# The matmuls of a gate tile and its up tile in alternating order, in the up projections of a transformer block

## The chip, the cores and the metric

The kernel runs on one core of a Trainium2 chip. Five engines work side by side and meet at semaphores: TensorE (PE, matmuls), VectorE (DVE), ScalarE (ACT), GpSimd (POOL) and SyncE (SP, which issues most transfers). The metric is the device time of one execution in microseconds (us), lower is better; a kernel's time is the median of its runs.

## The reference

Two blocks follow each other on a sequence of 512 tokens with 1024 features, in float32: one with two feed-forward networks around a mixer (attention over selected keys, and retention), and one with gated linear attention and a third feed-forward network. This case is about the three feed-forward networks. Each has two wide matrices side by side, "gate" and "up" (1024 to 2816 features), and a "down" matrix back to 1024. The third has a causal convolution of width 3 over the tokens ahead of the gating.

```
def swiglu(x, w_gate, w_up, w_down):
    return (jax.nn.silu(x @ w_gate) * (x @ w_up)) @ w_down
...
h = h + 0.5 * swiglu(rms_norm(h, ffn1_norm[i]), ffn1_w_gate[i], ffn1_w_up[i], ffn1_w_down[i])
...
def conv_ffn(x, w_up, conv_w, conv_b, w_down):
    s = x.shape[1]
    u = x @ w_up
    u_pad = jnp.pad(u, ((0, 0), (CONV_WIDTH - 1, 0), (0, 0)))
    u = sum(u_pad[:, j:j + s] * conv_w[j] for j in range(CONV_WIDTH)) + conv_b
    gate, up = jnp.split(u, 2, axis=-1)
    return (jax.nn.silu(gate) * up) @ w_down
```

## The kernel before, in words

Activations lie in SBUF with features on the 128 partitions and the 512 tokens along the row. All matmuls of the projections are made of three: operands are split into a high part (rounded to the matmul's format) and a low part (the rest), and the products low x high, high x low and high x high are added up in one PSUM bank (`mm3`, lines 1352 to 1357; the line of a matmul in the profile is one of 1355, 1356 and 1357 wherever it was called from).

A *slab* is the block of weights of one output tile: 8 blocks of 128 x 128, 512 KB. A ring of 4 slots (`RING`) holds raw slabs, their high parts and their low parts. SP loads raw slab n when the low part of slab n-4 is made. ACT makes the high part (line 613) when the raw slab has landed and the tile that used slab n-4 is done. POOL makes the low part (line 536) after it and increments `lo_ready`, on which TensorE waits. A *tile* is 128 output features x 512 tokens, 24 matmuls of 512 columns, in one of 4 PSUM banks (`BANKS`) in rotation; its last matmul increments `tile_done`, and the evacuation by DVE increments `tile_freed`, on which the tile four later waits.

An up projection (`ffn_up` in the program of the tensor engine) has 44 tiles, gate and up in turn, so 22 pairs. The first four tiles are written out; the others run in a loop of 10 rounds. The normalization is applied at the evacuation: the matmuls work on x times the gain, whose chunks are released by `u_ready`, and the factor `rstd` comes later, from a matmul with ones over the sums of squares (`sums(k)`), a root on ACT (line 639) and some steps on DVE (lines 905 to 914). `sums` stands behind tile 1 in the first up projection (k = 0) and behind tile 0 in the others (k = 2 and 5).

For a pair, DVE evacuates gate (line 927) and up (929), multiplies (932) after ACT's Silu (653), and makes the low part of the hidden chunk (934) after ACT's copy to its high part (656). In the third up projection DVE's list is longer, for gate and for up each: evacuation (951) and three steps of the convolution (953, 956, 959); then the product (963) and the low part (965). ACT's order in a pair p (`pair`, lines 645 to 657) is: the high part of slab 2p+4, Silu of the gate, the copy of the hidden chunk, the high part of slab 2p+5. After the 44 tiles the down projection (8 tiles of 66 matmuls, three slabs each) starts; it needs the first 18 hidden chunks at its start, and the last four one by one.

Every engine runs its own program in order; nothing reorders the matmuls.

Of the kernel before, what the change touches and what calls it, by code (L numbers as in the profile page):

```python
# [27 lines left out]
KD = D // P  # L28
# [15 lines left out]
RING = 4  # L44
BANKS = 4
# [135 lines left out]
def layer_program(nc, A, out):  # L181
# [12 lines left out]
    with ExitStack() as ctx:  # L194
# [8 lines left out]
        w_hi = sb("w_hi", [P, RING, SLAB], F32R)  # L203
        w_lo = sb("w_lo", [P, RING, SLAB], F32R)
        h = sb("h", [P, KD, S])
        u_hi = sb("u_hi", [P, KD, S], F32R)
        u_lo = sb("u_lo", [P, KD, S], F32R)
# [71 lines left out]
        acc = ctx.enter_context(nc.psum_tensor("acc", [P, BANKS, S], F32))  # L279
# [15 lines left out]
        lo_ready = sem("lo_ready")  # L295
        slab_used = sem("slab_used")
        tile_done = sem("tile_done")
        tile_freed = sem("tile_freed")

        u_hi_ready = sem("u_hi_ready")  # L300
        u_ready = sem("u_ready")
# [123 lines left out]
        def blk(b):  # L425
            return slice(b * P, (b + 1) * P)
# [909 lines left out]
        def _(pe):  # L1336
# [6 lines left out]
            def slabs_ready(n):  # L1343
                pe.wait_ge(lo_ready, n + 1)

            def free_bank(t):

                if t >= BANKS:
                    pe.wait_ge(tile_freed, t - BANKS + 1)
                return acc[:, t % BANKS, :]  # L1350

            def mm3(o, w, x_hi, x_lo, first, last):

                slot, columns = w
                pe.matmul(o, w_lo[:, slot, columns], x_hi, start=first, stop=False)  # L1355
                pe.matmul(o, w_hi[:, slot, columns], x_lo, start=False, stop=False)  # L1356
                return pe.matmul(o, w_hi[:, slot, columns], x_hi, start=False, stop=last)  # L1357
# [18 lines left out]
            def fm_tile(t, blocks, x_hi, x_lo, ready=None):  # L1376

                o = free_bank(t)
                seen = None
                for k, (n, b) in enumerate(blocks):  # L1380
                    if n != seen:
                        slabs_ready(n)
                        seen = n
                    if ready is not None:
                        pe.wait_ge(*ready(k))
                    last = mm3(o, (n % RING, blk(b)), x_hi[:, k, :], x_lo[:, k, :], k == 0, k == len(blocks) - 1)
                last.then_inc(tile_done, 1)
# [16 lines left out]
            def ffn_up(k, name):  # L1404

                n0, t0 = plan.first[name]
                for j in range(RING):
                    fm_tile(t0 + j, [(n0 + j, b) for b in range(KD)], u_hi, u_lo, (lambda c: (u_ready, KD * k + c + 1)) if j == 0 else None)
                    if j == (1 if k == 0 else 0):
                        sums(k)  # L1410
                with pe.Fori(1, 2 * KF // RING) as i:
                    for j in range(RING):
                        pe.wait_ge(lo_ready, i * RING + (n0 + j + 1))
                        pe.wait_ge(tile_freed, i * RING + (t0 + j - BANKS + 1))
                        for b in range(KD):
                            last = mm3(acc[:, (t0 + j) % BANKS, :], ((n0 + j) % RING, blk(b)), u_hi[:, b, :], u_lo[:, b, :], b == 0, b == KD - 1)
                        last.then_inc(tile_done, 1)

            def ffn_down(f, name):

# [22 lines left out]
            for step in MIX:  # L1443
# [5 lines left out]
                elif kind == "avw":  # L1449
                    o = free_bank(t)  # L1450
                    slabs_ready(n)
                    for k in range(KD):
                        last = mm3(o[0:AVW, :], (n % RING, slice(k * AVW, (k + 1) * AVW)), u_hi[:, k, :], u_lo[:, k, :], k == 0, k == KD - 1)
                    last.then_inc(tile_done, 1)
                elif kind == "avt":
# [3 lines left out]
                    for tt in range(NT):  # L1459
                        last = pe.transpose(aux[:, 3, tt * AVW:(tt + 1) * AVW], y_sq[0:AVW, 0, blk(tt)], ident[0:AVW, 0:AVW])  # L1460
# [6 lines left out]
                elif kind == "index":  # L1467
                    b = step[1]
# [3 lines left out]
                    for hd in range(2 * step[2], 2 * step[2] + 2):  # L1472
                        j = index_units[b] + hd
# [291 lines left out]
```

## Time and profile before

| | before |
|---|---|
| median of 3 runs | 1982.21 us (1982.18 to 1983.98) |
| profiled execution, span | 1981.7 us |
| PE busy | 95% (8492 matmuls, 8492 weight loads) |
| DVE / ACT / POOL busy | 49% / 35% / 43% |
| granted TensorE clock, mean | 0.977 |
| first / second / third up projection | about 8.5 to 256, 913 to 1154, 1579 to 1839 us |

The three up projections take 38% of the span. Busy shares are averages over stages: DVE is busy for about half of the kernel, but for 8 tenths and more of each slice in the third up projection. A matmul's busy time in the profile is longer than the distance to the next one, since they are pipelined; the pace is read from the starts.

### The profile page before, as it was taken

The page shows a single profiled execution, that of the slowest core. Times are in us where ns is not written, and L with a number is a line of the kernel's source. Part 1 is how long each engine was busy: PE and PEld are TensorE (multiplying, and loading weights), DVE is VectorE, ACT ScalarE, POOL GpSimd, SP SyncE. Part 2 cuts the span into 40 slices and gives each one's busy share as a digit, 9 for nine tenths or more (in the row PEclk, how much of TensorE's full clock was granted, in tenths as well). Part 3 has the DMA queues.
Part 4 walks back from the last instruction along what each step waited for, and adds up shares of the span by engine and source line. Part 5 has one row for each costly group of instructions (what it writes and reads, how often), then busy time and mean ns, then how long its engine had stood idle before and what let it go on. Part 6 is the DMA issues. An engine that isn't in the chain of part 4 may idle for free.

```text
span 1981.7 us, 23231 instructions
## 1 busy us (share of the span) xinstructions
PE 1884.6 (95%) x8492; PEld 1501.5 (76%) x8492; DVE 979.0 (49%) x1318; ACT 702.8 (35%) x923; POOL 842.3 (43%) x391
## 2 busy tenths in 40 slices
PE   7999999998889789999999999998999999999996
PEld 5888888786767457878888888876877887777785
DVE  6222244426777744334222222377756388888413
ACT  6434323313222444224443422335344433333221
POOL 4444444394547413444444444432333433344541
PEclk9999999998999899999999999998999999999998
DMA  4332333252222201222323233312222222222331
GB/s 165 105 106 86 101 95 95 85 154 70 80 69 71 79 32 64 96 85 96 102 89 106 84 98 97 103 55 84 72 69 66 94 85 85 85 85 82 109 95 43
DMA packets 52527, 174.52 MB, mean 88 GB/s; under 512 B 6368, under 2 KB 6752, under 8 KB 52464
## 3 DMA queue, kind: packets, MB, share of 16 engines
q1 hardware_dynamic: 52320, 173.40, 27.0%
q8 instruction: 41, 0.67, 0.1%
q10 hardware_dynamic: 144, 0.26, 0.0%
q14 instruction: 22, 0.18, 0.0%
HBM read 166.56 MB, written 2.10 MB: 85 GB/s over the span
## 4 chain that ended last, share of the span: by engine, by line
PE 61%; issue 21%; POOL 8%; DVE 7%; ACT 2%; DMA 0%; POOLq 0%; SPq 0%; DVEq 0%; ACTq 0%
PE acc L1355 19%; PE acc L1357 19%; PE acc L1356 18%; POOL w_lo L536 7%; PE acc L1538 1%; PE aux L1514 1%; PE aux L1495 1%; ACT w_hi L613 1%; DVE bias L1075 1%; DVE small L1074 1%; DVE y_sq L910 1%; PE aux L1476 0%; DVE probs L1114 0%; PE aux L1528 0%; DVE bias L1064 0%
## 5 line engine op out<-in xcount | busy, mean ns | idle before, releaser
L536 POOL TENSOR_TENSOR w_lo<-w_raw,w_hi 128x1024 fp32r<-128x1024 f32 (+1 forms) x317 | 754.1, 2384 | 1092.6 <-ACT w_hi L613 1092.5
L1355 PE MATMUL acc<-u_hi,w_lo 128*128 128x512 f32 x1592 | 634.6, 399 | 31.6 <-POOL w_lo L536 16.0
L1356 PE MATMUL acc<-u_lo,w_hi 128*128 128x512 f32 x1592 | 625.4, 393 | 0.0
L1357 PE MATMUL acc<-u_hi,w_hi 128*128 128x512 f32 x1592 | 625.0, 393 | 0.0
L613 ACT ACTIVATE w_hi<-w_raw 128x1024 fp32r<-128x1024 f32 (+1 forms) x317 | 325.0, 1034 | 566.9 <-PE acc L1357 506.8
L1355 PEld LDWEIGHTS acc<-u_hi,w_lo 128*128 128x128 f32 x1592 | 301.3, 189 | 114.6 <-issue 39.6
L1357 PEld LDWEIGHTS acc<-u_hi,w_hi 128*128 128x128 f32 x1592 | 300.7, 189 | 65.6 <-issue 0.8
L1356 PEld LDWEIGHTS acc<-u_lo,w_hi 128*128 128x128 f32 x1592 | 301.2, 189 | 64.3 <-issue 2.5
L1355 PE MATMUL acc<-hid_hi,w_lo 128*128 128x512 f32 x528 | 207.3, 393 | 2.1 <-POOL w_lo L536 2.1
L1357 PE MATMUL acc<-hid_hi,w_hi 128*128 128x512 f32 x528 | 207.3, 393 | 0.0
L1356 PE MATMUL acc<-hid_lo,w_hi 128*128 128x512 f32 x528 | 205.6, 389 | 0.0
L656 ACT ACTIVATE hid_hi<-tmp 128x512 f32 (+1 forms) x66 | 41.7, 632 | 272.5 <-DVE tmp L932 199.4
L989 DVE SCALAR_TENSOR_TENSOR h<-acc,h 128x512 f32<-128x512 f32 x24 | 16.6, 692 | 225.2 <-PE acc L1357 225.2
L929 DVE TENSOR_TENSOR tmp<-acc,rstd 128x512 f32<-128x512 f32 x44 | 30.4, 691 | 192.1 <-PE acc L1357 192.1
L1355 PEld LDWEIGHTS acc<-hid_hi,w_lo 128*128 128x128 f32 x528 | 99.2, 188 | 23.4 <-POOL w_lo L536 2.9
L1356 PEld LDWEIGHTS acc<-hid_lo,w_hi 128*128 128x128 f32 x528 | 99.1, 188 | 22.4
L1357 PEld LDWEIGHTS acc<-hid_hi,w_hi 128*128 128x128 f32 x528 | 99.2, 188 | 22.1
L956 DVE SCALAR_TENSOR_TENSOR tmp<-tmp,cols 128x512 f32<-128x512 f32 x44 | 72.4, 1647 | 6.6 <-DVE tmp L953 5.0
L927 DVE TENSOR_TENSOR tmp<-acc,rstd 128x512 f32<-128x512 f32 x44 | 30.4, 691 | 91.6 <-PE acc L1357 91.2
L1399 PE MATMUL acc<-w_hi,u_lo 128*128 128x256 f32 x256 | 72.9, 285 | 0.0
L1400 PE MATMUL acc<-w_lo,u_hi 128*128 128x256 f32 x256 | 72.4, 283 | 0.0
L1401 PE MATMUL acc<-w_hi,u_hi 128*128 128x256 f32 x256 | 72.4, 283 | 0.0
(271 smaller groups left out, 2115.9 us busy)
## 6 DMA issues: line engine op xcount, KB each, us to landing
w_raw<-in_w_up SPq DMA_DIRECT2D x132, 512.0 KB, 3.4
w_raw<-in_w_mix SPq DMA_DIRECT2D x69, 512.0 KB, 3.6
w_raw<-in_w_down SPq DMA_DIRECT2D x48, 512.0 KB, 3.5
w_raw<-in_w_gla SPq DMA_DIRECT2D x32, 512.0 KB, 3.4
w_raw<-in_w_down SPq DMA_DIRECT2D x24, 384.0 KB, 3.1
w_raw<-in_w_ple SPq DMA_DIRECT2D x10, 512.0 KB, 3.5
tmp<-tmp SPq DMA_DIRECT2D x36, 64.0 KB, 2.0
h<-in_xT SPq DMA_DIRECT2D x8, 256.0 KB, 6.0
```

Source lines behind the costliest of these rows:

```text
L536: pool.tensor_tensor(w_lo[:, slot, 0:width], w_raw[:, slot, 0:width], w_hi[:, slot, 0:width].bitcast(F32), ALU.subtract).then_inc(lo_ready, 1)
L613: act.activation(w_hi[:, slot, 0:width], w_raw[:, slot, 0:width], ACT.Copy).then_inc(hi_ready, 1)
L656: act.activation(hid_hi[:, i2 + b, :], src, ACT.Copy).then_inc(prod_hi, 1)
L927: dve.tensor_tensor(gate_t[:, b, :], acc[:, (t0 + 2 * b) % BANKS, :], rstd[:, :], ALU.mult).then_inc(tile_freed, 1)
L929: dve.tensor_tensor(up_t[:, b, :], acc[:, (t0 + 2 * b + 1) % BANKS, :], rstd[:, :], ALU.mult).then_inc(tile_freed, 1)
L956: dve.scalar_tensor_tensor(tmp[:, part, :], z[:, 1:1 + S], conv_col("conv_w1", i * 2, b, part * KF), tmp[:, part, :], ALU.mult, ALU.add).t ...
L1355: pe.matmul(o, w_lo[:, slot, columns], x_hi, start=first, stop=False)
L1356: pe.matmul(o, w_hi[:, slot, columns], x_lo, start=False, stop=False)
L1357: return pe.matmul(o, w_hi[:, slot, columns], x_hi, start=False, stop=last)
L1399: pe.matmul(o, u_lo[:, k, blk(tt)], w_hi[:, slot, columns], start=k == 0, stop=False)
L1400: pe.matmul(o, u_hi[:, k, blk(tt)], w_lo[:, slot, columns], start=False, stop=False)
L1401: last = pe.matmul(o, u_hi[:, k, blk(tt)], w_hi[:, slot, columns], start=False, stop=k == KD - 1)
```

## The change

Tiles are taken in pairs (0, 1) and (2, 3) of each round. For a pair, TensorE first waits for both slabs and both banks, and then issues, for each of the 8 blocks and each of the three products, one matmul of the gate tile and one of the up tile, in their two banks. Each tile's own matmuls keep their order. In the first up projection the first pair keeps the old order; in the others it alternates too, with the waits for the chunks of u, and `sums` then comes behind the pair. The last two matmuls of a pair release the two tiles. Nothing is changed on the other engines.

```
             def ffn_up(k, name):
 
                 n0, t0 = plan.first[name]
-                for j in range(RING):
-                    fm_tile(t0 + j, [(n0 + j, b) for b in range(KD)], u_hi, u_lo, (lambda c: (u_ready, KD * k + c + 1)) if j == 0 else None)
-                    if j == (1 if k == 0 else 0):
+
+                def pair_tiles(j, ready=None):
+                    for b in range(KD):
+                        if ready is not None:
+                            pe.wait_ge(u_ready, ready + b + 1)
+                        for part, operand, start, stop in ((w_lo, u_hi, b == 0, False), (w_hi, u_lo, False, False), (w_hi, u_hi, False, b == KD - 1)):
+                            for e in (j, j + 1):
+                                ins = pe.matmul(acc[:, (t0 + e) % BANKS, :], part[:, (n0 + e) % RING, blk(b)], operand[:, b, :], start=start, stop=stop)
+                                if stop:
+                                    ins.then_inc(tile_done, 1)
+
+                for j in (0, 2):
+                    if j == 0 and k == 0:
+                        for e in range(2):
+                            fm_tile(t0 + e, [(n0 + e, b) for b in range(KD)], u_hi, u_lo, (lambda c: (u_ready, c + 1)) if e == 0 else None)
+                    else:
+                        for e in (j, j + 1):
+                            slabs_ready(n0 + e)
+                            free_bank(t0 + e)
+                        pair_tiles(j, KD * k if j == 0 else None)
+                    if j == 0:
                         sums(k)
                 with pe.Fori(1, 2 * KF // RING) as i:
-                    for j in range(RING):
-                        pe.wait_ge(lo_ready, i * RING + (n0 + j + 1))
-                        pe.wait_ge(tile_freed, i * RING + (t0 + j - BANKS + 1))
-                        for b in range(KD):
-                            last = mm3(acc[:, (t0 + j) % BANKS, :], ((n0 + j) % RING, blk(b)), u_hi[:, b, :], u_lo[:, b, :], b == 0, b == KD - 1)
-                        last.then_inc(tile_done, 1)
+                    for j in (0, 2):
+                        for e in (j, j + 1):
+                            pe.wait_ge(lo_ready, i * RING + (n0 + e + 1))
+                            pe.wait_ge(tile_freed, i * RING + (t0 + e - BANKS + 1))
+                        pair_tiles(j)
```

## Rows read from the trace of the kernel before

**Rows 1.** The page, chain of work that ended last: share of each line.

```profile
PE acc L1355 19%; PE acc L1357 19%; PE acc L1356 18%; POOL w_lo L536 7%; PE acc L1538 1%; PE aux L1514 1%; PE aux L1495 1%; ACT w_hi L613 1%; DVE bias L1075 1%; DVE small L1074 1%; DVE y_sq L910 1%; PE aux L1476 0%; DVE probs L1114 0%; PE aux L1528 0%; DVE bias L1064 0%
```

**Rows 2.** Order of time, PE (start, duration, engine, operation): 256 columns, up2's tiles 4 and 43.

```profile
435.24 0.28 PE L1399 MATMUL acc<-w_hi,u_lo 128*128 128x256 f32 x1
435.36 0.28 PE L1400 MATMUL acc<-w_lo,u_hi 128*128 128x256 f32 x1
...
935.95 0.39 PE L1355 MATMUL acc<-u_hi,w_lo 128*128 128x512 f32 x1
...
1148.11 0.39 PE L1355 MATMUL acc<-u_hi,w_lo 128*128 128x512 f32 x1
```

**Rows 3.** Order of time, DVE and POOL, up2 under way: released together by tile_done.

```profile
963.35 0.69 DVE L927 TENSOR_TENSOR tmp<-acc,rstd 128x512 f32<-128x512 f32 x1 [2.31 <-PE acc L1357]
...
964.49 2.39 POOL L536 TENSOR_TENSOR w_lo<-w_raw,w_hi 128x1024 fp32r<-128x1024 f32 x1 [0.89 <-ACT w_hi L613]
```

**Rows 4.** Order of time, up2's entry: first evacuation, and slabs 5 and 6.

```profile
927.99 0.69 DVE L927 TENSOR_TENSOR tmp<-acc,rstd 128x512 f32<-128x512 f32 x1 [0.22 <-DVE rstd L914]
...
931.87 4.76 POOL L536 TENSOR_TENSOR w_lo<-w_raw,w_hi 128x1024 fp32r<-128x1024 f32 x2 [6.56 <-ACT w_hi L613]
```

**Rows 5.** Order of time, up1's entry: sums, tile 4; slab 3, slabs 5 to 8.

```profile
24.90 1.70 PE L1363 MATMUL aux<-ssum,ones 128*128 128x512 f32 x2 [2.37 <-DVE ssum L901]
...
38.40 0.39 PE L1355 MATMUL acc<-u_hi,w_lo 128*128 128x512 f32 x1
...
24.94 2.35 POOL L536 TENSOR_TENSOR w_lo<-w_raw,w_hi 128x1024 fp32r<-128x1024 f32 x1 [3.03 <-ACT w_hi L613]
...
40.08 10.47 POOL L536 TENSOR_TENSOR w_lo<-w_raw,w_hi 128x1024 fp32r<-128x1024 f32 x4 [6.57 <-ACT w_hi L613]
```

**Rows 6.** Order of time, up3's entry: evacuation, convolution; tile 4; slabs 5 and 6.

```profile
1593.39 0.69 DVE L951 TENSOR_TENSOR tmp<-acc,rstd 128x512 f32<-128x512 f32 x1
...
1595.08 0.75 DVE L956 SCALAR_TENSOR_TENSOR tmp<-tmp,cols 128x512 f32<-128x512 f32 x1 [0.16 <-DVE tmp L953]
...
1601.33 0.39 PE L1355 MATMUL acc<-u_hi,w_lo 128*128 128x512 f32 x1
...
1602.41 4.95 POOL L536 TENSOR_TENSOR w_lo<-w_raw,w_hi 128x1024 fp32r<-128x1024 f32 x2 [11.71 <-ACT w_hi L613]
```

**Rows 7.** Order of time, up3: DVE; POOL; PE's tile 11 and down's 25th matmul.

```profile
1599.92 0.69 DVE L963 TENSOR_TENSOR tmp<-tmp 128x512 f32<-128x512 f32 x1
...
1602.15 0.69 DVE L951 TENSOR_TENSOR tmp<-acc,rstd 128x512 f32<-128x512 f32 x1
...
1605.25 2.65 DVE L956 SCALAR_TENSOR_TENSOR tmp<-tmp,cols 128x512 f32<-128x512 f32 x1 [0.15 <-DVE tmp L953]
...
1611.97 0.69 DVE L963 TENSOR_TENSOR tmp<-tmp 128x512 f32<-128x512 f32 x1
...
1614.46 4.94 POOL L536 TENSOR_TENSOR w_lo<-w_raw,w_hi 128x1024 fp32r<-128x1024 f32 x2 [7.11 <-ACT w_hi L613]
...
1638.56 2.38 POOL L536 TENSOR_TENSOR w_lo<-w_raw,w_hi 128x1024 fp32r<-128x1024 f32 x1 [7.11 <-ACT w_hi L613]
...
1641.07 0.49 PE L1355 MATMUL acc<-u_hi,w_lo 128*128 128x512 f32 x1 [0.87 <-POOL w_lo L536]
...
1845.46 0.51 PE L1355 MATMUL acc<-hid_hi,w_lo 128*128 128x512 f32 x1 [0.60 <-POOL w_lo L536]
```

**Rows 8.** PE after two idles; stretches: PE, PEld, DVE, ACT, POOL busy, clock, DMA.

```profile
874.02 0.50 PE L1355 MATMUL acc<-mg_hi,w_lo 128*128 128x512 f32 x1 [1.53 <-DVE mg_lo L998]
...
1293.13 0.79 PE L1355 MATMUL acc<-p_hi,w_lo 128*128 128x512 f32 x1 [3.94 <-DVE tmp L1187]
...
25.00:28.50 3.50, 3.50 (x7) 2.19 (x8) 0.00 (x0) 1.81 (x2) 2.29 (x1) 0.54 0.02 6
1293.20:1298.20 5.00, 5.00 (x12) 3.94 (x13) 2.36 (x4) 2.00 (x3) 2.37 (x1) 0.50 0.04 5
...
874.00:876.00 2.00, 1.98 (x9) 1.64 (x10) 0.69 (x1) 0.26 (x1) 0.00 (x0) 1.00 0.05 18
```

## What I expect of the change, and why

> **What bounds the kernel now.** I read the page first, then the matmuls in order of time around the three up projections, then VectorE (DVE), ScalarE (ACT) and GpSimd (POOL) in the same stretches. The chain of waits is mostly TensorE, with POOL at L536 the largest item outside it [rows 1]. The matmuls in order of time say why. In the first two up projections TensorE never waits once it is under way: from tile 4 of up2 to tile 43 are 39 tiles in 212.16 us, 5.44 us a tile, 226.7 ns a matmul [rows 2]. So nothing on another engine counts there unless it comes late. The third up projection (up3) is different. Its DVE work per pair (convolution of gate and of up, product, split) takes 12.05 us in steady state (POOL's pairs of operations start at 1602.41 and 1614.46), against 10.88 us of matmuls, and TensorE sits 0.87 us before every second tile for a weight slab that POOL finishes 0.13 us before the matmul [rows 6, 7].
>
> How a slab travels matters for all that follows. ACT may make the high part of slab n only when tile n-4 is done, and POOL makes the low part after it. From release to POOL's start are 1.14 us, and POOL takes 2.4 us [rows 3]. ACT makes one slab of a pair at once and the other only after that pair's hidden chunk (Silu, product, copy). That second slab is late wherever DVE is late.
>
> **What is not changed.** The number of matmuls and weight loads (24 a tile), their shapes, the slabs, the DMAs and the evacuations stay. The order within a bank stays. The extra bookkeeping is nothing: the same two waits a tile, moved ahead of the pair.
>
> **Part 1, the pace of a matmul.** Each matmul now writes another bank than the one before. Before, that happens once in 24 matmuls. A 512-column matmul takes 226.7 ns and a 256-column one 120 ns [rows 2], so 256 columns cost 106.7 ns (2.4 GHz) and 13.3 ns a matmul are fixed. Ends of the cost: 13.3 ns less (the fixed part is something between two matmuls into one bank), or 3.5 ns more (an estimate: the intervals in up2 that cross from one bank to the next round to 0.23 us, the others average 226.5 ns). Tile spans of 5.44 us, crossing included, are nearest to no change: I take 0. The matmuls on which it would count are 960 in up1, 1008 in up2 and, at half weight (part 4), 528 in up3, so -33 to +9 us.
> The Trainium skill (TensorE: Matmul & The Clock Gate, "Wait — 56ns, not 53.3ns?") gives 512/2.4 + 2.5 = 216 ns a matmul in a row; this trace has 226.7. By the page at most 11 ns each could be won, 27 us in all.
>
> **Part 2, entry of up1.** The first pair and the statistics matmul keep their order. Tiles 2 and 3 now start together, and so wait for slab 3: 24.94 + 2.35 = 27.3 us in place of 25.6. They end by 40.5 at the latest, even at a low clock. Pair 2 needs slabs 4 and 5 at its start, where tile 4 alone started at 38.40 [rows 5]. Slab 5 is the second slab of pair 0; it hangs on the first rstd and is POOL's first operation from 40.08, ready at 42.5. Nothing in its chain moves. TensorE restarts at 42.55: +4.15 us. Before, tile 5 came 5.4 us later and covered this.
>
> **Part 3, entry of up2.** Here the statistics matmul now stands behind two tiles instead of one: 24 x 226.7 ns = 5.44 us later. The root, rstd, the first evacuation (927.99 before), the hidden chunk and slab 5 (931.87 + 2.4) all move with it [rows 4]. Slab 5 is ready at 939.7, and pair 2 starts at 939.8, where tile 4 started at 935.95 [rows 2]: +3.85 us. The chunks of u_lo are all there when asked for, so spreading the first tile gains nothing.
> After that the pairs run at 10.88 us. Pair 0 of up2 shows how late the second slab of a pair is when both tiles are there at once: 3.9 us from the gate evacuation to POOL's start, 2.4 for POOL [rows 4]. In the new order ACT and POOL make the first slab beside that, at most 2 us more: 8.3 us of the 10.88, so 2.6 us of cover, and no cost. Were it gone, each microsecond beyond would cost half a microsecond a pair (part 4). The last evacuations end at most 3 us later; their chunk is needed 14 us into the down projection.
>
> **The clock.** An idle of 1.53 us left the granted clock at 1.00. After an idle of 3.94 us it was 0.50 (1.2 GHz) for 12 matmuls, 0.2 us more each, 2.4 us in all; the 2.37 us idle in up1 was followed by 7 slow ones, 1.4 us [rows 5, 8]. Both new stalls (at least 2.1 us in up1, 3.8 in up2) are nearer to the idles that lost the clock. I take 2.1 us each, with 0 and 2.6 as ends.
>
> **Part 4, up3.** The entry moves as in up2. The first evacuation starts 5.44 later, at 1598.83, and slab 5 (1602.41 + 2.41) is ready at 1610.3 in place of 1604.8. Tile 4 started at 1601.33, so TensorE stands 9 us, restarts at 1610.35 and loses 2.3 us to the low clock [rows 6].
> Then a pair is a loop, counted from T, the start of its gate evacuation. Before: T to the product's start is 6.53 us without POOL beside it (1593.39 to 1599.92) and 9.82 with two POOL operations beside it (1602.15 to 1611.97). A DVE operation that starts under a POOL operation ends 0.54 us after POOL: L956 took 2.65 us instead of 0.75 [rows 6, 7]. In the new order both tiles are released together at T, so POOL's first slab runs from T+1.14 to T+3.53. L956 starts at T+1.7 and ends at T+4.08 instead of T+2.44: one collision in place of two, product at T+8.15. From the product's start to POOL's start are 2.49 us (1611.97 to 1614.46), then 2.41 for POOL and 0.13 to the matmul (1640.94 to 1641.07) [rows 7]: pair p+2 starts at T+13.15. Its own T comes 48 matmuls later, and 0.2 us for the semaphore (tile 9 of up2 starts at 963.15, the evacuation of tile 8 at 963.35 [rows 2, 3]) and 0.1 for a restart (an estimate: the first interval after a wait in up3 is 0.33 us): 11.19. Two pairs take 24.34 us, 12.17 a pair in place of 12.05. The saved collision (1.67) is eaten, because up no longer starts behind a gate already done: the path through DVE and the path through TensorE now follow each other.
> Pair 3 starts when pair 2 ends (1610.35 + 10.98 + 2.3 = 1623.6). Pair 21 is nine double steps on: 1842.7, and ends at 1853.65. The down projection's 25th matmul comes 5.5 us later, without the wait for a slab that it has now: 1859.2 against 1845.46 [rows 7], +13.7 us. Slabs 1 to 3 of down are there 1.8 us or more before their turn.
>
> **Sum.** 4.15 + 2.1 (up1) + 3.85 + 2.1 (up2) + 13.7 (up3) = 25.9 us. The profiled span is 1981.7; the median of the runs is 0.5 above it. 1981.7 + 25.9 + 0.5 = 2008.1 us.
>
> **Rivals.**
> A, the forecast: the pace stays, entries stall. 1999 to 2017: at the lower end no clock is lost in up1 and up2 (-4.2) and up3's entry costs half (-4.5), at the upper the pace costs 9 us. 55%.
> B, the other side: alternating banks removes what is fixed in a matmul. It takes 25.9/2496 = 10.4 ns of the 13.3 before the kernel is even; at all 13.3 it gives 25.9 - 33.2 = -7.3, 1975. For it: a matmul adds to the bank that the last one still writes. Against it: the crossings between tiles show no shorter interval. 12%.
> C: DVE gets past POOL in up3 without collision (6.53). Two pairs take 22.7, nine steps save 14.6: 1993; with the clock kept in up1 and up2, 1989; with up1's entry hidden as well, 1985. Needs POOL's slab to fall into the evacuation or behind the convolution. 14%, of it 4% within 0.2% of before.
> D: both collisions stay (9.82): 26.0 for two pairs, +15, 2023. Or the idle of 1.2 us before each pair of up3 costs the clock: one 2.1 us more in each double step, +19, 2027. Against the latter: 0.87 us per pair now, at full clock. 19%.
> The Trainium skill (TensorE: Matmul & The Clock Gate, "A second HAM failure mode: psum-queue depth-cycling") tells of small idles between groups in rotating banks that make the clock swing; it speaks for the second half of D, and the trace so far does not show it in up3.
> That the change does nothing is no rival: the order stands in the program, and matmuls run in order.
>
> **Chances.** Between 1978.2 and 1986.2 (0.2%, about what a measurement of this kernel can tell from no change) lies only the low end of C: 4%. Faster: B, 12%. Slower: 84%. The range 1988 to 2024 leaves out B, the low end of C and a few per cent of D.
>
> **What would show it.** Tiles 2 and 3 of up1 restart near 27.4, pair 2 near 42.5. In up2 a wait of 3.8 us before pair 2 for POOL L536, then 226.7 ns steadily. In up3 one wait of 9 us, then one of 1.2 before every pair instead of 0.87 before every second tile, DVE's L956 stretched and L953 at 0.55, DVE idle before each gate evacuation. Wrong would be: another interval than 226.7 ns in up2, or a loop in up3 clearly off 24.3 us.

## The result, and the profile after

| | before | after |
|---|---|---|
| median | 1982.98 us (1982.18 to 1983.98, 4 runs) | 2009.55 us (2004.05 to 2010.28, 4 runs) |
| profiled execution, its span | span 1981.7 us | 2009.1 us, span 2007.2 us |
| granted TensorE clock, mean | 0.977 | 0.973 |

The ratio after to before is 1.0127, with an interval of 1.0112 to 1.0141: slower, 26.6 us by the medians. The forecast was 2008.1 us in a range of 1988 to 2024.

The starts of the matmuls in order of time give a ledger by stage. The last matmul of the kernel starts at 1965.02 us before and at 1990.52 after, 25.5 us later. Forecasts are those of the prediction.

| stretch | before | after | difference | forecast |
|---|---|---|---|---|
| start to the first matmul of down1 (up1) | 256.00 | 259.68 | +3.7 | +6.25 |
| down1 and the mixer, nothing changed there | 657.27 | 660.37 | +3.1 | 0 |
| up2 | 240.28 | 246.77 | +6.5 | +5.95 |
| up2's end to up3's start, nothing changed there | 425.09 | 424.22 | -0.9 | 0 |
| up3 and down3 | 386.38 | 399.48 | +13.1 | +13.7 |

First the page of after: its span, the chain of work that ended last by engine and by line, and the costliest group of the new matmuls.

```profile
span 2007.2 us, 23232 instructions
...
PE 59%; issue 24%; POOL 9%; DVE 6%; ACT 1%; POOLq 0%; DVEq 0%; ACTq 0%
PE acc L1414 22%; PE acc L1355 11%; PE acc L1357 11%; PE acc L1356 10%; POOL w_lo L536 9%; PE acc L1555 1%; PE aux L1531 1%; PE aux L1512 1%; ACT w_hi L613 1%; DVE y_sq L910 0%; PE aux L1493 0%; DVE bias L1075 0%; DVE bias L1064 0%; PE acc L1399 0%; PE acc L1401 0%
...
L1414 PE MATMUL acc<-u_hi,w_lo 128*128 128x512 f32 x1040 | 326.0, 395 | 35.1 <-POOL w_lo L536 35.1
```

The chain looks like that of [rows 1], with POOL's share up from 7% to 9%. By the last line TensorE stood 35.1 us ahead of the first products of the alternating tiles, all of it for POOL's slabs. Before, all of its waits for POOL's slabs came to 18.0 us (view of the waits, before: who waited for whom, us in total, times, longest):

```profile
PE acc L1355 <- POOL w_lo L536: 18.0, 21, 1.5
```

So 17 of the 25.5 us are added waits for slabs. Next, where: after, order of time, PE (start, duration, [idle before <- releaser]). First pair 1 of up1 (tiles 2 and 3, which now wait for slab 3), then pair 2 of up1 and of up2 (their tile 4 is at 38.40 in [rows 5] and at 935.95 in [rows 2]), then up3 from its pair 2 on (tile 4 at 1601.33 in [rows 6]).

```profile
27.37 1.19 PE L1414 MATMUL acc<-u_hi,w_lo 128*128 128x512 f32 x2 [1.40 <-POOL w_lo L536]
...
41.94 0.72 PE L1414 MATMUL acc<-u_hi,w_lo 128*128 128x512 f32 x2 [2.04 <-POOL w_lo L536]
...
946.59 1.22 PE L1414 MATMUL acc<-u_hi,w_lo 128*128 128x512 f32 x2 [3.69 <-POOL w_lo L536]
...
1622.71 1.22 PE L1414 MATMUL acc<-u_hi,w_lo 128*128 128x512 f32 x2 [8.81 <-POOL w_lo L536]
...
1649.41 0.73 PE L1414 MATMUL acc<-u_hi,w_lo 128*128 128x512 f32 x2 [2.27 <-POOL w_lo L536]
...
1661.45 0.72 PE L1414 MATMUL acc<-u_hi,w_lo 128*128 128x512 f32 x2 [0.87 <-POOL w_lo L536]
...
1673.76 0.73 PE L1414 MATMUL acc<-u_hi,w_lo 128*128 128x512 f32 x2 [1.15 <-POOL w_lo L536]
...
1685.81 0.72 PE L1414 MATMUL acc<-u_hi,w_lo 128*128 128x512 f32 x2 [0.88 <-POOL w_lo L536]
...
1856.29 0.73 PE L1414 MATMUL acc<-u_hi,w_lo 128*128 128x512 f32 x2 [0.87 <-POOL w_lo L536]
```

One wait per entry for slab 5 (2.04, 3.69 and 8.81 us), and in up3 a wait ahead of every pair, 0.87 and about 1.13 in turn. Two pairs take 24.36 us (1661.45 to 1685.81). From 1685.81 to 1856.29 are 14 pairs in 170.48 us, 12.18 a pair. Before it was 12.03: from the tile at 1641.07 in [rows 7] to the one at 1749.36 are 9 pairs.

Stretches of after, with the columns of [rows 8]; the granted clock is the third number from the end.

```profile
41.90:45.00 3.10, 3.06 (x13) 2.55 (x14) 2.18 (x2) 2.50 (x3) 3.10 (x2) 1.00 0.50 169
946.59:949.60 3.01, 3.01 (x7) 2.43 (x8) 2.06 (x2) 2.42 (x3) 3.01 (x2) 0.50 0.54 173
1622.70:1628.00 5.30, 5.29 (x13) 4.19 (x14) 4.68 (x5) 0.63 (x1) 2.39 (x1) 0.52 0.58 196
1634.00:1860.00 226.00, 206.85 (x890) 165.48 (x890) 161.99 (x184) 81.78 (x90) 92.50 (x38) 1.00 0.26 85
```

The idle of 2.04 us in up1 kept the clock at 2.4 GHz, those of 3.69 and 8.81 us were followed by 1.2 GHz, as after the 3.94 us in [rows 8]. In up3, with an idle ahead of every pair for 226 us, it stayed at 1.00. Behind these two idles the matmuls start every 0.43 us instead of 0.227, until about 952 and 1628 us. That cost about 2.7 us in up2 and 2.5 in up3 (estimates from these intervals), some 5 of the 25.5 us. In up2 the wait (3.85 us over the pace) and the clock together are the 6.5 us of the ledger.

DVE and POOL of after, one pair of up3 in steady state. For POOL, x2 is two slabs in a row.

```profile
1672.43 0.69 DVE L951 TENSOR_TENSOR tmp<-acc,rstd 128x512 f32<-128x512 f32 x1 [1.35 <-PE acc L1414]
1673.31 0.60 DVE L953 TENSOR_SCALAR tmp<-tmp,cols 128x512 f32<-128x512 f32 x1 [0.19 <-DVE tmp L951]
1674.07 2.65 DVE L956 SCALAR_TENSOR_TENSOR tmp<-tmp,cols 128x512 f32<-128x512 f32 x1 [0.15 <-DVE tmp L953]
...
1680.78 0.69 DVE L963 TENSOR_TENSOR tmp<-tmp 128x512 f32<-128x512 f32 x1
...
1684.74 0.69 DVE L951 TENSOR_TENSOR tmp<-acc,rstd 128x512 f32<-128x512 f32 x1 [1.62 <-PE acc L1414]
...
1671.25 4.92 POOL L536 TENSOR_TENSOR w_lo<-w_raw,w_hi 128x1024 fp32r<-128x1024 f32 x2 [7.10 <-ACT w_hi L613]
1683.28 2.40 POOL L536 TENSOR_TENSOR w_lo<-w_raw,w_hi 128x1024 fp32r<-128x1024 f32 x1 [7.11 <-ACT w_hi L613]
1685.88 2.63 POOL L536 TENSOR_TENSOR w_lo<-w_raw,w_hi 128x1024 fp32r<-128x1024 f32 x1 [0.20 <-ACT w_hi L613]
```

DVE, which before never stood ahead of a gate evacuation, is now idle 1.35 to 1.62 us ahead of each gate evacuation, waiting for the pair that TensorE has just been given. From T (1672.43) to the product (1680.78) are 8.35 us with one stretched step, L956. The groups by line show it over the whole loop, after (1640 to 1860 us) and then before (1640 to 1840): count, busy, mean ns, idle before.

```profile
L956 DVE SCALAR_TENSOR_TENSOR tmp<-tmp,cols 128x512 f32<-128x512 f32 x37 | 63.9, 1728 | 5.6 <-DVE tmp L953 4.3
...
L951 DVE TENSOR_TENSOR tmp<-acc,rstd 128x512 f32<-128x512 f32 x36 | 24.8, 689 | 25.6 <-PE acc L1414 25.6
L953 DVE TENSOR_SCALAR tmp<-tmp,cols 128x512 f32<-128x512 f32 x36 | 21.2, 589 | 7.5 <-DVE tmp L951 7.5
```

```profile
L956 DVE SCALAR_TENSOR_TENSOR tmp<-tmp,cols 128x512 f32<-128x512 f32 x34 | 57.9, 1703 | 5.1 <-DVE tmp L953 3.8
L953 DVE TENSOR_SCALAR tmp<-tmp,cols 128x512 f32<-128x512 f32 x34 | 43.3, 1274 | 7.1 <-DVE tmp L951 7.1
...
L951 DVE TENSOR_TENSOR tmp<-acc,rstd 128x512 f32<-128x512 f32 x33 | 22.6, 684 | 0.0
```

L953 (the mean of a gate and an up step) fell from 1274 to 589 ns: the second collision with POOL is gone. The idle of L951 rose from 0 to 25.6 us: the gain is given back as waiting.

### The profile page after: what moved, and what is told of

It reads as the page before. It is cut to its first block, busy times and chain, and to the rows that moved or that the text cites. A ratio compares the mean times of both kernels' runs of the same rounds, so it can differ in the third digit from the quotient of the medians.

```text
span 2007.2 us, 23232 instructions
## 1 busy us (share of the span) xinstructions
PE 1892.1 (94%) x8492; PEld 1506.7 (75%) x8492; DVE 995.6 (50%) x1318; ACT 704.3 (35%) x923; POOL 842.9 (42%) x391
## 4 chain that ended last, share of the span: by engine, by line
PE 59%; issue 24%; POOL 9%; DVE 6%; ACT 1%; POOLq 0%; DVEq 0%; ACTq 0%
PE acc L1414 22%; PE acc L1355 11%; PE acc L1357 11%; PE acc L1356 10%; POOL w_lo L536 9%; PE acc L1555 1%; PE aux L1531 1%; PE aux L1512 1%; ACT w_hi L613 1%; DVE y_sq L910 0%; PE aux L1493 0%; DVE bias L1075 0%; DVE bias L1064 0%; PE acc L1399 0%; PE acc L1401 0%
## 5 line engine op out<-in xcount | busy, mean ns | idle before, releaser
L1414 PE MATMUL acc<-u_hi,w_lo 128*128 128x512 f32 x1040 | 326.0, 395 | 35.1 <-POOL w_lo L536 35.1
L1414 PE MATMUL acc<-u_lo,w_hi 128*128 128x512 f32 x1040 | 322.7, 392 | 0.0
L1414 PE MATMUL acc<-u_hi,w_hi 128*128 128x512 f32 x1040 | 322.3, 391 | 0.0
L1414 PEld LDWEIGHTS acc<-u_hi,w_lo 128*128 128x128 f32 x1040 | 195.3, 190 | 84.9 <-DVE tmp L951 24.0
L1355 PE MATMUL acc<-u_hi,w_lo 128*128 128x512 f32 (+2 forms) x552 | 226.8, 411 | 16.1 <-DVE u_lo L893 8.6
L1356 PE MATMUL acc<-u_lo,w_hi 128*128 128x512 f32 (+2 forms) x552 | 220.8, 400 | 0.0
L1357 PE MATMUL acc<-u_hi,w_hi 128*128 128x512 f32 (+2 forms) x552 | 220.3, 399 | 0.0
L1355 PEld LDWEIGHTS acc<-u_hi,w_lo 128*128 128x128 f32 (+2 forms) x552 | 106.1, 192 | 50.5 <-issue 16.6
L1357 PEld LDWEIGHTS acc<-u_hi,w_hi 128*128 128x128 f32 (+2 forms) x552 | 105.7, 192 | 25.1 <-issue 0.8
L1356 PEld LDWEIGHTS acc<-u_lo,w_hi 128*128 128x128 f32 (+2 forms) x552 | 106.2, 192 | 23.3 <-issue 1.5
## 6 DMA issues: line engine op xcount, KB each, us to landing
h<-in_xT SPq DMA_DIRECT2D x8, 256.0 KB, 5.9
```

The lines of the kernel that those rows point to most:

```text
L1414: ins = pe.matmul(acc[:, (t0 + e) % BANKS, :], part[:, (n0 + e) % RING, blk(b)], operand[:, b, :], start=start, stop=stop)
```

## The experiments

The theory (A): the pace of the matmuls is unchanged; the cost is that two tiles are released together and asked for together, so that slabs come late at the entries and up3's loop goes through DVE and TensorE one after the other. The rivals: the alternation itself costs or gains time per matmul; the moved statistics matmul costs it all; the clock. Each ratio is to the kernel before on the same chip. Where a stretch is named, it is that of the ledger above.

### Which projection, which part

**e3_up2_loop_only**: alternation in up2's loop alone, from pair 2 on, entry as before.

```
+            def ffn_up_alt(k, name):
...
+                for j in range(RING):
+                    fm_tile(t0 + j, [(n0 + j, b) for b in range(KD)], u_hi, u_lo, ...)
...
+                with pe.Fori(1, 2 * KF // RING) as i:
...
+                        pair_tiles(j)
...
+                (ffn_up_alt if k == 2 else ffn_up_seq)(k, name)
```

> Only the loop of the second up projection alternates (40 tiles, 960 matmuls), behind an entry in the old order. Theory: no wait for a slab, 226.7 ns a matmul, ratio 1.000 within 0.1%. Rival (alternating banks removes a fixed part of a matmul, up to 13.3 ns): down to -12.8 us, 0.9935. Rival (3.5 ns more each): +3.4 us, 1.0017.

Measured: 1983.06 us, ratio 1.0001 [0.9992, 1.001]. Up2 took 240.29 us, against 240.28. Gate evacuations in up2, first clean pair and last:

```profile
957.00 0.69 DVE L927 TENSOR_TENSOR tmp<-acc,rstd 128x512 f32<-128x512 f32 x1 [5.19 <-PE acc L1429]
...
1152.84 0.69 DVE L927 TENSOR_TENSOR tmp<-acc,rstd 128x512 f32<-128x512 f32 x1 [5.22 <-PE acc L1429]
```

18 pairs in 195.84 us are 10.88 each, 226.7 ns a matmul, as in [rows 2]. Rival B wanted 12.8 us less in this stage (960 matmuls at 13.3 ns); it is excluded, and so is a price per matmul: the stage differs by 0.01 us. In this stage the whole cost of the change comes with its entry.

**e2_up3_only**: the whole change in up3 alone (`k == 5` in the line above).

> Only the third up projection alternates. Theory: up3 and the down projection behind it carry 13.1 us of the changed kernel's 25.5, ratio 1.0066, with one wait of 9 us and then about 1.2 us before every pair. Rival (a cost of each alternated matmul): a third of the change, 1.004.

Measured: 1995.95 us, ratio 1.0066 [1.0051, 1.0082]; up3 and down3 399.83 us, +13.45. Half of the loss is up3's, as forecast, with the entry's wait of 8.82 us and the low clock (0.50 from 1608 to 1613 us) unchanged by what happens in the other projections.

**e1_entry_old**: the first four tiles of each up projection as before, `sums` behind tile 1 or 0 included; the loop alternates.

```
-                for j in (0, 2): ... pair_tiles(j, ...)
-                    if j == 0:
+                for j in range(RING):
+                    fm_tile(t0 + j, [(n0 + j, b) for b in range(KD)], u_hi, u_lo, ...)
+                    if j == (1 if k == 0 else 0):
                         sums(k)
```

> The first four tiles of every up projection in the old order, with the statistics matmul where it was; the loop alternates. Theory (late slabs, no change of pace): up1 still waits for slab 5 ahead of pair 2, +3.5 us; up2 has slab 5 at 934.3, before 935.95, so +0; up3 waits 3.5 us instead of 9 for slab 5 and its loop then runs at 24.3 us for two pairs, all 5.4 us earlier than in the changed kernel, +8 us with the down projection. In all +11 us, ratio 1.006. Rival (alternating costs time by itself, in every matmul): near the changed kernel's 1.013, since 40 of 44 tiles still alternate.

Measured: 1998.06 us, ratio 1.0074 [1.0059, 1.009]. Up2 cost nothing, up3 and down3 +6.8 us. Its waits for pair 2, in up1 and in up3:

```profile
42.70 1.21 PE L1414 MATMUL acc<-u_hi,w_lo 128*128 128x512 f32 x2 [4.20 <-POOL w_lo L536]
...
1611.44 0.72 PE L1414 MATMUL acc<-u_hi,w_lo 128*128 128x512 f32 x2 [3.37 <-POOL w_lo L536]
```

The total is some 3 us over what I expected: up1 lost 7.3 us, more than in after itself (3.7), because the longer idle took the clock as well (1.2 GHz from 42.7 to 48.9 us), while up3 and down3 lost a microsecond less than expected. So up1's wait doesn't come from the entry's order: the loop's first pair asks for slab 5 when tile 4 starts, whatever stands before it.

**e12_seq_late_sums**: the kernel before, with `sums` behind tile 1 in every up projection (in the first it stood there already). Nothing alternates.

```
-                    if j == (1 if k == 0 else 0):
+                    if j == 1:
                         sums(k)
```

> The kernel before with one edit: in up2 and up3 the statistics matmul comes behind tile 1 instead of tile 0, as the change has it. Theory: in up2 slab 5 is at 939.7 and is asked for at 941.4, so +0; in up3 VectorE's chain starts 5.4 us later and is what binds, +5.4 us, with a wait for slab 5 of some 3.5 us: ratio 1.0027. Rival (the place of the statistics does not matter): 1.000.

Measured: 1988.33 us, ratio 1.002 [1.0011, 1.003]; up2 +0.0, up3 and down3 +5.3.

```profile
1607.98 0.79 PE L1355 MATMUL acc<-u_hi,w_lo 128*128 128x512 f32 x1 [3.37 <-POOL w_lo L536]
```

The late statistics alone make tile 5 of up3 wait, and the clock falls behind that (0.50 from 1608 to 1613 us). In up2, whose DVE list is short, the same delay is fully covered. e12 (+5.3, the late statistics alone) and e1 (+6.8, the common start and the loop alone) add up to 12.1 of the 13.1 us of up3 and down3. What the last microsecond is stays open; the clock is lost in all three. In up2 it is otherwise: e12 and e1 each cost nothing there, and the two together 6.5 us, because each fits into the slack that the other takes.

### Is it the slab's order or the release of both tiles?

**e4_alt_early_slabs**: after, but ACT makes the high parts of both slabs of a pair before Silu, so that the second no longer hangs on the hidden chunk. **e5_seq_early_slabs**: the same edit on the kernel before.

```
                         split_a()
+                        split_b()
...
                     act.activation(hid_hi[:, i2 + b, :], src, ACT.Copy).then_inc(prod_hi, 1)
-                    split_b()
```

> The changed kernel, but ScalarE makes the high parts of both slabs of a pair at once when the pair is done, ahead of the Silu. Theory (the cost is the second slab's hand-over): no wait for slab 5 in up1 and up2, 1.3 us left in up1 for slab 3; up3 loses its 24.3 us loop and is bound by VectorE at 12.05 us a pair, behind a start 5.4 us later: +6 us in all, ratio 1.003. Rival (alternating itself costs): stays at 1.013.

> The kernel before with both slabs of a pair made by ScalarE ahead of the Silu, the edit that took the changed kernel from 1.013 to 1.0105. Theory: in up1 and up2 nothing waits for them either way; in up3 VectorE sets the pace, and the table load that ScalarE makes at each second pair moves GpSimd's pair of operations 1.3 us on, where it falls on two long steps of the convolution: 12.43 us a pair in place of 12.05, as measured with alternation, +8 us, 1.004. Rival (early slabs are good for any order): 1.000 or below.

Measured: e4 2003.67 us, ratio 1.0105 [1.0089, 1.012]; e5 1993.67 us, 1.0051 [1.0033, 1.0069]. e5 met its forecast, e4 missed: I expected most of the loss back. In up2 it came back (241.37 us, +1.1 instead of +6.5), which shows that up2's cost runs through the second slab's place in ACT's list. In up1 the wait for slab 5 is gone and the 1.40 us for slab 3 are left, as forecast; but the clock stayed at 1.2 GHz behind them until 33.3 us, and up1 took 258.7 us. In up3 it didn't (+12.6 instead of +13.1). e4's matmuls in up3 say what took the slab's place, and its DVE what that costs:

```profile
1660.16 0.73 PE L1415 MATMUL acc<-u_hi,w_lo 128*128 128x512 f32 x2 [1.65 <-DVE tmp L952]
...
1672.18 0.73 PE L1415 MATMUL acc<-u_hi,w_lo 128*128 128x512 f32 x2 [0.84 <-DVE tmp L952]
...
1678.60 2.96 DVE L957 SCALAR_TENSOR_TENSOR tmp<-tmp,cols 128x512 f32<-128x512 f32 x1 [0.15 <-DVE tmp L954]
1681.71 2.65 DVE L960 SCALAR_TENSOR_TENSOR tmp<-tmp,cols 128x512 f32<-128x512 f32 x1 [0.15 <-DVE tmp L957]
```

TensorE now waits for DVE to free the up tile's bank (L952), which it needs at the start of the pair instead of half a pair later. POOL's two slabs stretch two steps in every pair (L957 and L960 in one pair, L954 and L957 in the next), and two pairs take 24.86 us; e5, in the old order, has the same two collisions and 24.82. In both DVE never stands ahead of an evacuation: with early slabs it is the bound of up3, and the order of the matmuls hardly matters for it.

**e6_alt_late_slab** and **e7_seq_late_slab**: in up3 ACT does two extra copies (1.1 us) ahead of the second slab, on after and on before.

```
+                    if conv:
+                        act.activation(side[:, 0, :], u_hi[:, 0, :].bitcast(F32), ACT.Copy)
+                        act.activation(side[:, 1, :], u_hi[:, 0, :].bitcast(F32), ACT.Copy)
                     split_b()
```

> The changed kernel with two more copies of 128x512 on ScalarE in each pair of up3 (1.07 us together, their result is used by nothing), between the hidden chunk's copy and the second slab's high part. Theory (pair p+2 waits for that slab, in a loop of two pairs): each double step is 1.07 us longer, nine or ten of them, +10 us on the changed kernel, ratio about 1.018. Rival (up3 bound by VectorE's work as before): 0 to +5 us on the changed kernel.

> The same two copies in the kernel before. Theory (there VectorE's work sets the pace, and a later slab only shifts where GpSimd falls on it): 0 to +5 us, ratio 1.000 to 1.0026. Rival (the slab's path binds there as well): one late slab a pair, up to +1.07 us a pair, +20 us, 1.010.

Measured: e6 2032.52 us, ratio 1.0246 [1.0229, 1.0263], two pairs 27.2 us in place of 24.36; e7 1993.89 us, 1.0047 [1.003, 1.0064], 12.46 us a pair in place of 12.03. The direction was right, both sizes were too small: e6 had been put at 1.018, e7 at 1.0026 at most, and both are outside their intervals. The delay doesn't only add itself, it moves POOL over another DVE step and makes idles long enough to lose the clock. PE and DVE of e6, first while it loses the clock, then between 1798 and 1837 us, where it doesn't:

```profile
1704.72 0.77 PE L1417 MATMUL acc<-u_hi,w_lo 128*128 128x512 f32 x2 [3.57 <-POOL w_lo L536]
...
1809.65 0.69 DVE L954 TENSOR_TENSOR tmp<-acc,rstd 128x512 f32<-128x512 f32 x1 [1.64 <-PE acc L1417]
1810.53 1.32 DVE L956 TENSOR_SCALAR tmp<-tmp,cols 128x512 f32<-128x512 f32 x1 [0.19 <-DVE tmp L954]
1812.01 2.66 DVE L959 SCALAR_TENSOR_TENSOR tmp<-tmp,cols 128x512 f32<-128x512 f32 x1 [0.15 <-DVE tmp L956]
...
1818.74 0.69 DVE L966 TENSOR_TENSOR tmp<-tmp 128x512 f32<-128x512 f32 x1
```

From 1798.66 us on, over three pairs, two pairs take 26.1 us, 1.74 more than in after. T to the product is 9.09 us (1809.65 to 1818.74) instead of 8.37, since POOL, which works off the late slab and the next one in a row from 1809.21 us on, now reaches into L956 (a step of 0.55 us by itself) as well as into L959; 0.72 of that and 1.07 of delay are 1.79. Before 1731 us the idle is 3.57 us in every second pair, each time with the clock at 0.6 for some 3 us after it, and two pairs take 27.2. In both, what is added between T and the slab comes out at the end once per two pairs: the loop is one chain of slab, pair, DVE, slab. Behind the wait at 1837.8 us, of 1.88 us like the three before it, the clock was lost once more. In the old order (e7) the delay is not in the chain. DVE, which never stands ahead of an evacuation there, bounds the loop. Its idles within a pair are those of before, and the stretched steps are now the second and third of the convolution (L959 and L962 of e7, 2.6 us each) instead of the first and second: the 0.43 us a pair come from the moved collisions.

**e8_alt_half_skew**: alternating, but the up tile runs half a tile (4 blocks) behind the gate tile, and claims its slab and bank there.

```
+                    for s in range(KD + KD // 2):
+                        if s == KD // 2:
+                            claim_tile(j + 1)
...
+                            for e, b in ((j, s), (j + 1, s - KD // 2)):
+                                if 0 <= b < KD:
```

> The changed kernel with the up tile half a tile behind: blocks 0 to 3 of gate alone, then gate 4 to 7 and up 0 to 3 in alternation, then up 4 to 7 alone; the up tile's slab and bank are waited for at its own first matmul. Theory (what costs is that both tiles are asked for and released together): waits of 1.3 us in up1, 1.0 in up2, VectorE bound again in up3, behind a start 5.4 us later: +8 us, ratio 1.004. Rival (the alternation as such): half of the matmuls alternate, half of the change, 1.0065, with the loop of 24.3 us in up3 unchanged.

Measured: 1993.22 us, ratio 1.0045 [1.0027, 1.0062]; up3 and down3 +5.4. PE in up3, entry and loop:

```profile
1616.15 1.22 PE L1419 MATMUL acc<-u_hi,w_lo 128*128 128x512 f32 x2 [6.11 <-POOL w_lo L536]
...
1676.33 0.73 PE L1419 MATMUL acc<-u_hi,w_lo 128*128 128x512 f32 x2 [0.87 <-POOL w_lo L536]
1688.35 0.73 PE L1419 MATMUL acc<-u_hi,w_lo 128*128 128x512 f32 x2 [0.86 <-POOL w_lo L536]
```

A pair is back at 12.02 us, with half of its matmuls still alternating between two banks. DVE is never idle ahead of a gate evacuation there and has both of its collisions again, as before. The entries' waits shrank by 2.7 us each in up2 and up3 (to 0.99 and 6.11); in up1 it is 1.77. The ratio is the one forecast. What is left in up3 and down3, +5.4, is what the late statistics cost alone (e12, +5.3). So in up3 it is not the alternation that costs, but the lost distance between the two tiles, and the late statistics.

### Versions that beat both

**e9_seq_dve_early_gate**: the kernel before; in up3 DVE evacuates the next gate tile after the product, while ACT makes the copy that the low part waits for. **e10_alt_dve_early_gate**: the same on after.

```
                     dve.tensor_tensor(tmp[:, 1, :], tmp[:, 0, :], tmp[:, 1, :], ALU.mult).then_inc(prod_ready, 1)
+                    if more:
+                        evacuate(i4, 2 * b + 2)
                     dve.wait_ge(prod_hi, i2 + (f * KF + b + 1))
```

> The kernel before, but in up3 VectorE evacuates the next pair's gate tile while it would wait for ScalarE's copy of the hidden chunk, ahead of the low part. Theory (up3 before is bound by VectorE at 12.05 us a pair): 0.7 to 0.9 us less a pair, -15 us or somewhat less, ratio 0.992 to 0.995. Rival (up3 before is bound by slabs or banks): no change, 1.000.

> The changed kernel with the edit on VectorE that took the kernel before to 0.9943 (the next gate tile is evacuated ahead of the hidden chunk's low part). Theory: with alternation VectorE waits for the pair, so there is no gate tile to take early, and the loop through the second slab (24.35 us for two pairs) does not contain the step: within 2 us of the changed kernel, 1.012 to 1.014. Rival (VectorE binds there too): 10 us less than the changed kernel, 1.007.

Measured: e9 1972.44 us, ratio 0.9943 [0.9926, 0.996], 11.58 us a pair; e10 2022.6 us, 1.0188 [1.0167, 1.0208], 12.92 a pair. I expected e10 to be no better than after; it was worse by 0.6%, for a reason that I had not foreseen. DVE of e10:

```profile
1700.29 0.69 DVE L949 TENSOR_TENSOR tmp<-acc,rstd 128x512 f32<-128x512 f32 x1 [2.37 <-PE acc L1428]
1700.90 1.72 DVE L971 TENSOR_TENSOR hid_lo<-tmp,hid_hi 128x512 f32 x1
1702.54 2.63 DVE L957 TENSOR_SCALAR tmp<-tmp,cols 128x512 f32<-128x512 f32 x1
```

In alternation the next gate tile isn't ready at the product; DVE stands 2.37 us for it with the low part (L971) queued behind the wait. That step then lies inside the next pair's chain and meets POOL there.

**e11_seq_timed_slabs**: e9, with the second slab's high part right after Silu, and POOL's low part of it held until the product, so that the two slabs don't both fall on the convolution.

```
                         act.activation(tmp[:, 0, :], tmp[:, 0, :], ACT.Silu).then_inc(gate_act, 1)
+                        split_b()
...
+                    pool.wait_ge(prod_ready, i * 2 + (2 * KF + b + 1))
+                    lo_part((n + 1) % RING, SLAB, i * RING + (n + 2))
```

> The version at 0.9943, and in up3 ScalarE makes the second slab's high part right behind the Silu, while GpSimd makes its low part only once the product has started (a wait for the product). Theory (VectorE's steps are held up while GpSimd runs, except evacuations out of PSUM): the second slab's operation falls on the evacuation and on the wait for the hidden chunk, 2.3 us of hold-up a pair in place of 3.4, so a pair takes 10.9 us (TensorE's own 10.88) in place of 11.58, -14 us, ratio 0.987. Rival (the hold-up only moves to other steps): 0.994.

Measured: 1964.79 us, ratio 0.9897 [0.9875, 0.992], between the forecast of 0.987, which lies just outside, and the rival's 0.994; up3 and down3 368.07 us, 18.3 less than before. In all of up3 TensorE waits for nothing (1575 to 1834 us); its next wait is 1.16 us for the last hidden chunks. DVE of e11:

```profile
1712.06 2.18 DVE L986 TENSOR_TENSOR hid_lo<-tmp,hid_hi 128x512 f32 x1 [0.33 <-ACT hid_hi L670]
1714.17 2.62 DVE L972 TENSOR_SCALAR tmp<-tmp,cols 128x512 f32<-128x512 f32 x1
1716.94 0.75 DVE L975 SCALAR_TENSOR_TENSOR tmp<-tmp,cols 128x512 f32<-128x512 f32 x1 [0.15 <-DVE tmp L972]
```

Both of POOL's slabs still cost DVE two stretched steps, so a pair takes DVE 11.23 us (products are 11.1 and 11.3 us apart in turn) and not the 10.9 expected. Against e9 the slabs are in time for TensorE, which waited about 0.4 us a pair there and waits for none here. e11 made three moves at once (e9's, ACT's and POOL's), and no run parts the last two.

## Why the prediction was right, point by point

**The pace (part 1)**: right. I took 0 between ends of -33 and +9 us; e3 measured 0.0 in up2 with an interval of about 2 us either way. The Trainium skill (TensorE: Matmul & The Clock Gate, "Wait — 56ns, not 53.3ns?") gives 216 ns a matmul in a row. Measured are 226.7 ns with one bank and with two, so the surplus over that figure isn't the accumulation into the same bank; what it is stays open.

**Up1's entry (part 2)**: the mechanism right, the size too large against this execution of before. Pair 1 waited for slab 3 and started at 27.37 for 27.4. The wait for slab 5 came, 2.04 us long; pair 2 started at 41.94, not at 42.55, since POOL began slab 5 at 39.44 instead of 40.08, a time that lies between 39.3 and 40.2 in the runs that leave up1 as it was. The 2.1 us for the clock didn't come: the prediction took them because the idle was "nearer to the idles that lost the clock", and idles of this length are no ground for that (e10 kept the clock behind 2.56 us at this place; e1, with 4.20 us, lost it). The +3.7 itself hangs on one execution of before, which had lost the clock at the statistics matmul (25.3 us) and took 256.0 us. Six other profiled executions with up1 unchanged (e2, e3, e7, e9, e11, e12) kept it there and took 254.2 to 255.1 us. Against those after's 259.7 is a loss of 4.6 to 5.5 us, nearer to the forecast of 6.25.

**Up2's entry (part 3)**: right. 3.69 us of wait (excess over the pace 3.85, the forecast number), then the clock at 1.2 GHz until about 952 us (2.7 us lost, for 2.1); +6.5 for 5.95. After it up2 runs without another wait, as the forecast cover said; e4 confirms the cause, since taking ACT's second slab out of the hidden chunk's shadow brings 5.4 of the 6.5 us back. The prediction had put the move of `sums` first here. e12 shows that this alone costs nothing in up2, and e1 that the common start alone costs nothing: it takes both.

**Up3 (part 4)**: right in mechanism and nearly so in its terms. Entry: 8.81 us for 9, low clock after it. Loop: 24.36 us for 24.34, made of terms that each were off a little and cancelled. T to the product took 8.35 to 8.38 us for 8.15, since POOL is done with the slab beside it 3.74 to 3.77 us after T, not 3.53 (it starts right behind the slab before it, at 1685.88 with 2.63 us instead of 2.39). From the pair's start to its own T are 10.98 us (1661.45 to 1672.43) for 11.19. One collision in place of two, and DVE idle ahead of each gate evacuation, both as written. What the terms missed is pair 4, which waited 2.27 us instead of 1.2; the last pair so started 1.2 us later after up3's start than forecast. What set that right is a gain that was forecast by half: both waits of before in the down projection (0.60 us at its 25th matmul, which the sum has, and 1.46 us at 1856.83, which it has not) are gone, 2.6 us back.

**The sum**: 25.9 us forecast, 25.5 at the last matmul. But 3.1 us of these come from down1 and the mixer, where nothing was changed and for which I had 0, and they stand in for the 2.5 us that up1 fell short of its term in the ledger. Down1 takes 120.64 us in every profile, so they lie in the mixer. The granted clock there is 0.95 before (390 to 910 us) and 0.94 after (394 to 917 us), with low stretches that differ from run to run; after's own runs spread over 6 us. The profiled execution of e7, whose program up to up3 is that of before, took 661.3 us from down1 to up2, 4.0 more than before; the others with up1's entry in the old order (before, e1, e2, e3, e5, e9, e11, e12) took 656.5 to 657.8, and the five in which it alternates (after, e4, e6, e8, e10) 658.6 to 660.5. So a difference of 3 us comes without any change, and whether the change adds to it isn't shown. So the sum was right by its mechanisms to within about 3 us, and to 0.4 us by luck.

**The rivals**: B is excluded by e3. C didn't come: POOL's slab falls on L956 in every pair. The first half of D (both collisions stay) didn't come in after, but e6 shows how near it was: with 1.07 us more on ACT a second step is stretched again, though a shorter one. The second half of D, the clock in up3, is excluded for after by the stretch at 1.00 above, and e6, with 3.57 us of idle in every second pair, shows what it costs when it comes; the Trainium skill (the same page, "A second HAM failure mode: psum-queue depth-cycling") tells of small idles between groups in cycling banks that make the clock swing, and idles of 0.87 to 1.15 us ahead of every pair did not do that here.

## What to carry to other kernels

When two tiles are interleaved, count what they are released from and asked for together: the matmuls cost the same, but the buffers of both must be there at the start and come free only at the end, which takes half a pair of slack from whatever ran through the second. Here that cost nothing in the loops of the first two up projections and the difference between 12.03 and 12.18 us a pair in the third; the larger part of the loss came at the entries. In a loop with little slack look for the chain buffer, tile, evacuation, buffer and keep its two halves staggered. Before work is reordered on the engine that waits, look at the order on the engine it waits for: here a few steps moved on DVE, ACT and POOL gave 1%, where the reordering on TensorE lost 1.3%.

## What the runs showed of the hardware that I had not expected

- A convolution step of DVE that starts while POOL works ends a fixed time after POOL does, 0.55 us where it reads two tensors from SBUF: L956 of after ends at 1676.72 (1674.07 + 2.65), POOL's pair at 1676.17. L953, which reads one tensor, is held too (2.62 us for 0.55 in e11, L972 there); it ends 0.28 us after POOL. The evacuations from PSUM aren't held: 689 ns on average in after's loop. So whether POOL falls on an evacuation or on a convolution step is worth about 2 us. The Trainium skill (SBUF — State Buffer, "SBUF: two separate sides") tells of a port pair that a GpSimd operation, or a DVE operation with two inputs from SBUF or in a two-port mode, locks for its whole length. L956 and the evacuations, which have one input from PSUM, agree with this; in which mode L953 runs no profile shows.
- The idle that costs the clock isn't told by its length alone in these runs. In the up projections every idle of 3.25 us or more was followed by 1.2 GHz, and none of up to 1.77 us was, but for the one of 1.40 us in after and e4 that follows one of 2.3 us at once. In between both happened. At the statistics matmul of up1 idles of 2.37 us (before), 2.38 (e8) and 2.17 (e1) lost the clock, idles of 2.38 (e5, e11) and 2.33 to 2.37 (e2, e3, e7, e9, e12) did not. In up3 two of five waits of about 2.25 us lost it in e5, two of three of 2.74 us and one of four of 1.88 us in e6; the 2.27 us of after and the 2.68 us of e10 did not. What tells these apart stays open.
